# The intra-chunk score products of a hybrid token mixer: low levels by quarters into a compact tile, in five groups

## The reference, cut to what matters

```python
b = cumsum(gi, axis=2)                                   # log decay, one per channel
rel_decay = where(causal, exp(b[:, :, :, None] - b[:, :, None]), 0)
scores  = einsum('bhid,bhjd,bhijd->bhij', qi, ki, rel_decay)
o       = einsum('bhij,bhje->bhie', scores, vi) + einsum('bhcd,bhde->bhce', qi * exp(b), state)
state   = state * exp(b_last)[..., None] + einsum('bhcd,bhce->bhde', ki * exp(b_last - b), vi)
```

## Time and profile before

| | |
|---|---|
| median of 3 runs | 2037.15 us |
| profiled execution | span 2040.4 us from the first to the last instruction; no time of its own beside the span is given |
| TensorE busy | 1925.7 us (94%) |
| VectorE busy | 1472.5 us (72%) |
| chunk 0 of the mixers | 608.23 to 660.34 us of the span |
| chunks 1 to 6 | 660.34 to 1009.49 us |
| VectorE, all 56 copies of the levels' scores | 50.0 us |

### The profile page before, as it was taken

How to read it: one execution, slowest core, us unless ns; L and a number is a source line. 1 busy time by engine, 2 the same in 40 slices (tenths; PEclk the granted TensorE clock), 3 DMA queues, 4 the chain that set the end, 5 groups by cost and what they waited for, 6 DMA issues and landing times. The chain is left out here.

```text
span 2040.4 us, 26797 instructions
## 1 busy us (share of the span) xinstructions
PE 1925.7 (94%) x10602; PEld 1576.7 (77%) x10603; DVE 1472.5 (72%) x1687; ACT 1048.0 (51%) x1234; POOL 218.3 (11%) x173
## 2 busy tenths in 40 slices
PE   6999999999999999999998999995999999999993
PEld 5789888888977777777776888874788888888881
DVE  5876467667227888788775656556889988999875
ACT  5234344444224545444444334223777887888763
POOL 3310000000030000000001000012122222222210
PEclk9999999999999999999998999997999999999996
DMA  5242332432355557656537654543999999999986
GB/s 168 86 145 73 114 104 97 131 104 93 107 145 158 151 160 168 167 127 152 160 115 282 206 204 182 229 178 138 349 376 384 389 386 385 389 386 387 387 331 259
DMA packets 212415, 436.11 MB, mean 214 GB/s; under 512 B 28018, under 2 KB 151042, under 8 KB 184770
## 3 DMA queue, kind: packets, MB, share of 16 engines
q1 hardware_dynamic: 179394, 355.68, 50.3%
q10 hardware_dynamic: 20864, 53.49, 7.5%
q0 software_dynamic: 12032, 25.22, 3.2%
HBM read 369.67 MB, written 81.43 MB: 221 GB/s over the span
## 5 line engine op out<-in xcount | busy, mean ns | idle before, releaser
L1602 PE MATMUL psum<-h_hi,l_hi 128*128 128x512 f32 x384 | 158.5, 413 | 4.9 <-PEq L58 3.3
L1602 PE MATMUL psum<-h_lo,l_hi 128*128 128x512 f32 x384 | 159.8, 416 | 0.0
L1602 PE MATMUL psum<-h_hi,l_lo 128*128 128x512 f32 x384 | 157.9, 411 | 0.0
L2741 DVE TENSOR_TENSOR gu_lo<-up_raw,gu_hi 128x2048 fp32r<-128x2048 f32 x64 | 146.3, 2288 | 13.2 <-ACT gu_hi L2684 13.2
L2684 ACT CAST gu_hi<-up_raw 128x2048 fp32r<-128x2048 f32 x64 | 122.1, 1909 | 35.0 <-PE u_ps L2813 35.0
L1258 ACT COPY l_out<-psum 128x512 f32<-128x512 f32 x48 | 28.1, 585 | 170.3 <-PE psum L1602 162.3
L2457 PE MATMUL mpsum<-y_hi,wb_hi 128*128 128x512 f32 x256 | 103.3, 403 | 10.1 <-DVE y_lo L2217 9.1
L2813 PE MATMUL g_ps<-gu_hi,xeT_hi 128*128 128x512 f32 x256 | 105.0, 410 | 5.8 <-DVE xeT_lo L2750 5.8
L806 DVE TENSOR_TENSOR w_lo<-w_raw,w_hi 128x512 fp32r<-128x512 f32 x90 | 61.9, 689 | 65.5 <-ACT w_hi L662 65.5
L662 ACT CAST w_hi<-w_raw 128x512 fp32r<-128x512 f32 x90 | 55.7, 622 | 91.9 <-PE ps L931 91.4
L2457 PE MATMUL mpsum<-y_lo,wb_hi 128*128 128x512 f32 x256 | 101.7, 397 | 0.0
(11 more groups left out here) (465 smaller groups left out, 5419.0 us busy)
## 6 DMA issues: line engine op xcount, KB each, us to landing
up_raw<-moe SPq DMA_DIRECT2D x62, 1024.0 KB, 8.1
gate_raw_a<-moe SPq DMA_DIRECT2D x33, 1024.0 KB, 8.4
gate_raw<-moe SPq DMA_DIRECT2D x33, 1024.0 KB, 8.4
dn_raw_a<-moe SPq DMA_DIRECT2D x31, 1024.0 KB, 7.2
dn_raw<-moe SPq DMA_DIRECT2D x31, 1024.0 KB, 8.0
w_raw<-w_in SPq DMA_DIRECT2D x26, 1024.0 KB, 6.1
l_raw<-w_gates ACTq DMA_DIRECT2D x24, 512.0 KB, 5.4
s_gates<-l_out ACTq DMA_DIRECT2D x48, 256.0 KB, 4.0
```

Source lines behind the costliest of these rows:

```text
L1602: ins = nc.tensor.matmul(psum[:, bank, :], w[t % 2][:, k, :], x[:, k, half * 512:half * 512 + 512], start=i == 0, stop=i == LATE_MM - 1, s ...
L2741: nc.vector.tensor_tensor(gu_lo[p][:], gu_raw[p][:], gu_hi[p][:].bitcast(F32), ALU.subtract).then_inc(gu_ready, 1)
```

## The change: what it does

1. **Five groups instead of nine.** Levels 1 and 2, 3 and 4, and 5 and 6 are put next to each other on TensorE, with one semaphore step for both; the diagonal is one step. The late products that stood between them are in longer stretches: 8, 24, 16, 16, 8, 16 before the transposes of k, where it was 8 eight times and then 16. There are still 120 in a chunk.
2. **Quarters.** Levels 2 to 6 and the diagonal are computed for 4 quarters of 32 keys instead of 2 halves of 64: 24 matmuls with 32 weight columns, of 16 (or twice 16) moving columns. Level 1 has its two blocks of 32 keys. Level 0 stays.
3. **A compact tile.** Levels 2 to 6 and the diagonal are copied under a mask into `near` [128, 8, 32] instead of `score`: 128 columns a level and 256 for the diagonal. The blocks of levels 0 and 1 go into `score` by plain copies (1 of 64 partitions, 2 of 32).
4. **GpSimd** then moves the four diagonal blocks of `near` into `score`, four copies of 32 partitions x 8 x 32 a chunk, and the output product waits for them as well (`near_moved`).
5. **Order.** On VectorE the diagonal comes first and factors 1 after it; factors 3 and 4 come right ahead of `cbm`, `dec` 6 and 7 and `late(h0)` behind it. On TensorE `ssm_state` comes right after B.C, and `ssm_means` after the transposes of B, with levels 3 and 4 behind them. At the start of the stage five masks are built instead of seven, each reduced to one quarter.

```diff
+    SLOT_OF = (1, 2, 2, 3, 3, 4, 4)
+    COL_OF = (0, 0, 256, 0, 128, 0, 128)
+    NS = SLOT_OF[-1] + 1
...
+            for c in range(NCH):                     # GpSimd
+                pool.wait_ge(score_ready, NS * (c + 1))
+                for r in range(4):
+                    rs = slice(r * QUART, (r + 1) * QUART)
+                    nc.gpsimd.tensor_copy(score[rs, :, rs], near[rs, :, :]).then_inc(near_moved, 1)
...
+                def far_in(lv):                      # VectorE
+                    s, at, h = SLOT_OF[lv], COL_OF[lv], LEVELS[lv]
+                    dve.wait_ge(sc_ready, NS * c + s + 1)
+                    if c:
+                        dve.wait_ge(o_ready, c)
+                    for k in range(0, CH, 2 * h):
+                        ins = nc.vector.tensor_copy(score[k:k + h, :, k + h:k + 2 * h],
+                                                    sc_ps[s % 2][k:k + h, at:at + NH * h].rearrange("p (a h) -> p a h", h=h))
+                    if lv == 0:
+                        ins.then_inc(score_ready, 1)
+                def near_in(lv):
+                    s, at, h = SLOT_OF[lv], COL_OF[lv], LEVELS[lv]
+                    dve.wait_ge(sc_ready, NS * c + s + 1)
+                    v = lambda x: x.rearrange("p (n h) -> p n h", h=h)
+                    ins = nc.vector.copy_predicated(near[:].rearrange("p a (n w) -> p (a n) w", w=2 * h)[:, :, h:2 * h],
+                                                    v(mask[lv][:]), v(sc_ps[s % 2][:, at:at + NH * QUART // 2]))
+                    if lv % 2:
+                        own.link(ins)
+                    else:
+                        ins.then_inc(score_ready, 1)
+                        dve.wait_ge(score_ready, NS * c + s + 1)
...
                 factors(0)
+                diagonal_in()
+                dec(i0 + 3)
                 factors(1)
...
-                scores_in(2)
-                dec(i0 + 6)
+                far_in(1)
+                near_in(2)
+                factors(3)
                 factors(4)
-                late(h0)
                 dve.wait_ge(cb_ready, c + 1)
                 tt(cbm[:], ...)
+                dec(i0 + 6)
+                dec(i0 + 7)
+                late(h0)
                 if c:
                     ssm_state(c - 1)
-                scores_in(3)
-                dec(i0 + 7)
+                near_in(3)
+                near_in(4)
                 factors(5)
                 late(h0 + 1)
-                scores_in(4)
                 factors(6)
                 ... # xdt, dec 8, k and q of the state as before
-                scores_in(6)
+                near_in(5)
+                near_in(6)
...
             def level(c, lv):                        # TensorE
+                s, at, h = SLOT_OF[lv], COL_OF[lv], LEVELS[lv]
+                n = NS * c + s
                 pe.wait_ge(qk_ready, NE * c + lv + 1)
-                pe.wait_ge(score_ready, NS * c + lv + 1)
+                if n > 1:
+                    pe.wait_ge(score_ready, n - 1)
+                rows, cols, each = (h, h, 2 * h) if lv < FIRST_MASK else (QUART, QUART // 2, QUART)
+                out = sc_ps[s % 2][:, at:at + NH * cols].rearrange("p (a n) -> p a n", n=cols)
                 for a in range(CT):
+                    head, q2 = pairs_of_heads(ql, a)
+                    for i, k in enumerate(range(0, CH, each)):
+                        ins = nc.tensor.matmul(out[k:k + rows, head:head + q2.shape[1], :],
+                                               k_lv[lv % 2][:, a * CH + k:a * CH + k + rows],
+                                               q2[:, :, i * cols:(i + 1) * cols], start=True, stop=True, skip_group_check=True)
+                if lv % 2 == 0:
+                    ins.then_inc(sc_ready, 1)
...
                 level(c, 0)
-                fill(SLOT)
+                fill(3 * SLOT)
                 level(c, 1)
-                fill(SLOT)
                 level(c, 2)
                 ... # B.C of the SSM
-                fill(SLOT)
-                level(c, 3)
                 if c:
                     ssm_state(c - 1)
-                fill(SLOT)
-                if c:
-                    ssm_means(c - 1)
+                fill(2 * SLOT)
                 pe.wait_ge(cbm_ready, c + 1)
                 ... # transposes of B
-                fill(SLOT)
+                if c:
+                    ssm_means(c - 1)
+                level(c, 3)
                 level(c, 4)
-                fill(SLOT)
+                fill(2 * SLOT)
                 ... # transposes of x
                 fill(SLOT)
                 level(c, 5)
-                fill(SLOT)
                 level(c, 6)
                 fill(2 * SLOT)
...
                 pe.wait_ge(score_ready, NS * c + NS)
+                pe.wait_ge(near_moved, 4 * c + 4)
```

More of the change, by code:

```diff
@@ L1003, in mixers @@
         mask_f = sb("mask_f", [P, HALF])
-        mask = many(NL, "mask", [P, NH * HALF], U8)
-        mask_d = sb("mask_d", [P, 4 * CH], U8)
+        mask_q = sb("mask_q", [P, QUART])
+        mask = {lv: sb(f"mask{lv}", [P, NH * QUART // 2], U8) for lv in range(FIRST_MASK, NL)}
+        mask_d = sb("mask_d", [P, NH * QUART], U8)
         tri = sb("tri", [P, CH])
@@ L1050, in mixers @@
         score_ready = sem("score_ready")
+        near_moved = sem("near_moved")
         eb6_ready = sem("eb6_ready")
@@ L1215, in _ @@
             n = 0
[L1216 removed]
+            for lv in range(FIRST_MASK, NL):
+                h = LEVELS[lv]
                 nb = CH // (2 * h)
[L1218 to L1219 removed]
+                if lv > FIRST_MASK:
+                    pool.wait_ge(mask_ready, lv - FIRST_MASK)
                 nc.gpsimd.memset(mask_f[:], 1.0).then_inc(mask_sem, 1)
@@ L1502, in body @@
                     late(3)
-                scores_in(0)
+                far_in(0)
                 factors(2)
+                dec(i0 + 5)
                 if c:
                     intra_in(c - 1, 1)
[L1507 to L1510, removed]
                     x_weighted(c - 1)
@@ L1613, in heads, with pairs_of_heads @@
                     yield GLA_HEADS + h, 4 + h, 2 + h, slice(0, P)
+            def pairs_of_heads(q, a):
+                return (2 * a, q[:, a:4:2, :]) if a < 2 else (a + 2, q[:, a + 2:a + 3, :])
             def level(c, lv):
+                s, at, h = SLOT_OF[lv], COL_OF[lv], LEVELS[lv]
+                n = NS * c + s
                 pe.wait_ge(qk_ready, NE * c + lv + 1)
-                pe.wait_ge(score_ready, NS * c + lv + 1)
+                if n > 1:
+                    pe.wait_ge(score_ready, n - 1)
                 ql = q_lv[lv % 2][:].rearrange("p (a n) -> p a n", n=HALF)
-                out = sc_ps[lv % 2].rearrange("p (a n) -> p a n", n=HALF)
+                rows, cols, each = (h, h, 2 * h) if lv < FIRST_MASK else (QUART, QUART // 2, QUART)
+                out = sc_ps[s % 2][:, at:at + NH * cols].rearrange("p (a n) -> p a n", n=cols)
                 for a in range(CT):
[L1623 to L1629, removed]
+                    head, q2 = pairs_of_heads(ql, a)
[5 more added lines that the diff above has]
+                    ins.then_inc(sc_ready, 1)
             def diagonal(c):
@@ L1636, in diagonal @@
                     pe.wait_ge(inter_used, c)
[L1637 to L1642, removed]
-                    ins.then_inc(sc_ready, 1)
+                out = sc_ps[0][:, 0:NH * QUART].rearrange("p (a n) -> p a n", n=QUART)
+                for a in range(CT):
+                    head, q2 = pairs_of_heads(q_in[b], a)
+                    for r in range(4):
+                        rs = slice(r * QUART, (r + 1) * QUART)
+                        ins = nc.tensor.matmul(out[rs, head:head + q2.shape[1], :], k_in[b][:, a, rs], q2[:, :, rs],
+                                               start=True, stop=True, skip_group_check=True)
+                ins.then_inc(sc_ready, 1)
             def ssm_state(c):
@@ L1729, in body @@
                 for h, qa, a, r in heads():
-                    nc.tensor.matmul(o_ps[:, h * CH:(h + 1) * CH], v_in[:, h, :], score[:, h * CH:(h + 1) * CH], start=True, stop=False)
+                    nc.tensor.matmul(o_ps[:, h * CH:(h + 1) * CH], v_in[:, h, :], score[:, h, :], start=True, stop=False)
                     ins = nc.tensor.matmul(o_ps[:, h * CH:(h + 1) * CH], state[:, a, :], q_in[b][:, qa, :], start=False, stop=True)
```

48 lines of the change are left out of this document (21 added, 27 removed).

## The result

| | before | after |
|---|---|---|
| median of 20 runs, us | 2037.64 | 2046.16 |
| lowest to highest | 2034.06 to 2045.44 | 2039.36 to 2052.72 |
| ratio, 95% interval | | 1.0029 (1.0019 to 1.0039) |
| profiled execution: span, granted clock | 2040.4, 0.975 | 2045.0, 0.969 |
| mixers, first diagonal to last (chunks 0 to 6), us | 401.3 | 400.8 |

A forecast was written before the change was run, and what follows sets the result against it. TensorE's own list, plus waits at the transposes of B, was taken as the bound. Seven chunks at 2.4 us less (16.8) plus chunk 0's 3.1 made 20 us: 2037 to 2017, range 2003 to 2033, the forecast's own 2008 to 2026.

The forecast's parts named there:

- B at T+22.0: TensorE reaches the transposes of B 22.0 us after the chunk's start, when the chain load, `wd`, `cbm` ends.
- a second part of 32.1 before the clock: From the transposes of B to the next chunk, TensorE's list takes 32.1 us, from 33.7 without the clock's 1.7.
- chunk 0's 3.1 of gain: Chunk 0, without earlier SSM work or a wait for `cbm`, gains 3.1 us through levels, alternations and a shorter stop.
- A level's cost: Levels 2 to 6 on TensorE: 12 sets of four matmuls take 0.50 us a level instead of 0.82.
- records, not columns: Rival: a matmul record costs 34 ns in any width, a level 1.64 us; 2055, mild form 2041; chance 0.13.
- four no faster than two: Rival: four narrow matmuls side by side gain nothing, a level stays at 0.82 us; 2028; chance 0.13.
- TensorE idles 2.8 there, as today: Ahead of the transposes of B, TensorE is ready at 19.2 us but waits 2.8 us for `cbm`.
- the clock's 1.7: Half-clock TensorE behind the wait at the transposes of B: 1.7 us lost, charged to every chunk.
- The two alternations: Behind the transposes of B, two switches between late products and small groups go, saving 0.6 us at 0.3 each.
- the stop in the late products stands in place of its second wait, 0.3 less: Chunk 0: a 0.8 us stop among 24 late products replaces a 1.1 us wait for `l_out`, 0.3 less.
- cost 0: GpSimd's four copies, some 1.7 us a chunk, end before TensorE's output products ask, so they cost nothing.
- GpSimd late: Rival: GpSimd copies excluded by VectorE's multiplication end 0.8 us after TensorE asks; 6 us in seven chunks, 2023; chance 0.10.

The follow-up runs named there:

- e15: e13 with VectorE's copies of levels 5 and 6 ahead of the multiplications of k and q: 2012.2 us, ratio 0.9877.
- e1: The changed kernel with `wd` and its wait for `load_bb` behind `cbm` on VectorE: 2027.4 us, ratio 0.9933.
- e10: The changed kernel with the late products dealt 8, 16, 24 instead of 8, 24, 16 in chunk 0 alone: 2035.9 us, ratio 0.9979.
- e13: e8 with ScalarE's copy of the second half also sooner, ahead of the two wide exponentials: 2045.9 us, ratio 1.003.
- e9: The kernel before the change, unedited, profiled once more: one execution, 2033.6 us, its mixers 395.4 us.
- e3: The changed kernel without the four GpSimd copies and the waits for them, those score blocks missing from its result: 2040.3 us, ratio 1.0006.
- both edits: The changed kernel with `wd` and its load wait behind `cbm`, and late products dealt 8, 16, 24 in all chunks: 2023.4 us, ratio 0.992.
- e8: The kernel with both edits, ScalarE's copy of the half ending ahead of the transposes of B moved before W's first eight differences: 2022.6 us, ratio 0.9914.
- e11: The kernel with both edits, on VectorE `cbm` ahead of level 4's factors and the intra products' sum ahead of `dec` 5: 2022.5 us, ratio 0.992.
- e12: The kernel with both edits, without the four GpSimd copies and their waits, those score blocks missing from its result: 2021.2 us, ratio 0.9911.

## Why the prediction was wrong

Forecast: eight chunks 20 us shorter in all, 17.5 of them in the 401.3 us of chunks 0 to 6. Measured there: 401.2 on average of two profiles. The waits and the cost of the packed matmuls were foreseen; what failed are three terms of the sum, B at T+22.0, a second part of 32.1 before the clock, and chunk 0's 3.1 of gain, and the single profile that it started from.

- **A level's cost: right.** 0.50 a level was forecast. Levels 3 and 4 together take 1.01 (the 96 records from 684.36 to 685.37 in e15's chunk 1), levels 5 and 6 1.02; the diagonal takes 0.66 against 0.53. A level's records are 11 ns apart. The Trainium skill, "TensorE: Matmul & The Clock Gate", section "Wait — 56ns, not 53.3ns?", has a floor near 25 ns, by which the change would have been lost at once; for these records, four tiles side by side, the measurement decides against it. The rivals "records, not columns" and "four no faster than two" are out.
- **The first part, T to B: the step "TensorE idles 2.8 there, as today".** B was put at T+22.0, and came at T+21.0 to 23.8, 22.6 on average of seven, with 3.3 us of waiting each. Three of the seven lie beyond the T+23 that the forecast had named as a sign of being wrong. The transfer was issued 0.2 later than forecast (T+1.8), took 14.9 to 17.7 us, 16.5 on average, instead of 16.3, and the chain behind `wd` 4.3 instead of 4.1. Each is a small miss, and together they are 0.6 a chunk, 4 us: the mechanism was foreseen and its size nearly. What was missed is a question that was not put: what it would be worth to take `wd` out of the chain. e1: 17 to 19 us.
- **The second part: the step "That makes 32.1".** With the clock's 1.7, 33.8 was forecast; 34.6 was measured (six chunks), 5 us in all. The two chunks of the changed kernel in which the clock stayed at 1.00 behind B have 33.2, so the list was 1.1 too short. Today's list was put at 33.7, and chunk 5 before the change, at a clock of 1.00, has 34.0. The means cost 1.8 instead of 1.3. The two alternations gave 0.4 instead of 0.6. The clock cost less than forecast, 1.4 on average instead of 1.7: nothing in two chunks, about 1.6 in two, and over 2 in chunks 5 and 6, where it stayed low for twice as long.
- **Chunk 0: the step "the stop in the late products stands in place of its second wait, 0.3 less".** The stop was priced at 0.8 by a copy that waits for nothing. In chunk 4 it costs 0.93 (`l_out` waited for 0.77), so that was right; in chunk 0 ScalarE stood before the copy for its earlier store (1.43 us of idling) and TensorE waited 2.67. With the 3.58 us stop in level 5, which nothing had announced, chunk 0 is 4.1 us longer instead of 3.1 shorter. e10 shows that dealing chunk 0's late products otherwise takes both away: 9 to 10 us by the medians, 7 in chunk 0 of its profile.
- **GpSimd: "cost 0", right for the wrong reason.** TensorE did not wait for the copies. 1.7 us in all was forecast for them, done 2.5 us ahead of need. The copies take 3.8 and end at B+18.65 in chunk 4 (879.95), 0.4 us ahead of the output products. e13 took that reserve away and lost 23 us. The rival "GpSimd late" had the mechanism, and its chance of 0.10 was too small for whoever edits next.
- **The base.** The sum was taken off one profile whose mixers were 6 us longer than in the second profile of the same kernel (e9), 3 longer than the average of the two. A sum of 20 us should have carried such differences in its range.

By sizes: 4 (first part), 5 (second part), 7 (chunk 0) and 3 (the base) are 19 of the 28 to 29 us between 2017 and the medians of 2044.7 and 2046.2. 1 to 3 more are the starting point, 2037 from three runs where later series had 2037.6 to 2040.2. The last 6 to 9 are not placed; the stage begins up to 6 us earlier or later from one profile to the next (607.6 to 613.9), in both kernels alike.

What makes the stop of 3.58 us in level 5 is open as well. It stood in two profiles of the changed kernel and in e3, and in none that deals chunk 0's late products 8, 16, 24, though the levels are as dense there; so density alone is not it. e1 keeps the old dealing and has no such stop, but there TensorE waited 2.40 us for ScalarE's copy behind levels 3 and 4, and its chunk 0 is as long. No experiment isolates the cause.

## What to carry to other kernels

When a stage is a chain through a transfer, shorten nothing on it before looking which instruction waits for the transfer, and who is only queued behind that one: moving a `wd` of 0.17 us gave 17 us or more, and without that move some 2 us a chunk less of TensorE's work gave nothing. Keep two profiles of the kernel before when the effect is a few us a stage: here they differed by 6. Edits that each give nothing may be three queues that hold one point in turn; take them together (beside both edits, e8, e11, e12 and e13 gave 1, 1, 2 and -23 us, of which only the last is clear of none, and e15, one move more than e13, 11). Whatever is put on GpSimd beside a busy VectorE wants a reserve for each VectorE instruction that it can meet: the four copies took 6.0 us in chunk 0 of the changed kernel and 5.2 in two chunks of e15, where several of them met one.

## What the runs showed of the hardware that was not expected

A GpSimd copy of 32x256 takes 0.39 us alone and 2.44 us when VectorE's 2.29 us multiplication of two SBUF operands stands beside it. The changed kernel, chunk 4, the first, third and fourth copy, and that multiplication:
```profile
876.15 0.39 POOL L1249 COPY score<-near 32x256 f32<-32x256 f32 x1 [54.41 <-DVE near L1515]
...
877.05 2.44 POOL L1249 COPY score<-near 32x256 f32<-32x256 f32 x1
...
879.55 0.40 POOL L1249 COPY score<-near 32x256 f32<-32x256 f32 x1
...
876.94 2.29 DVE L1578 TENSOR_TENSOR dn_raw_a<-dn_raw_a,cbm 128x2048 f32<-128x2048 f32 x1 [0.85 <-ACT dn_raw_a L1338]
```
The third copy ends 0.26 us after the multiplication does (879.49 and 879.23). By the rule of the Trainium skill, "SBUF — State Buffer", section "SBUF: two separate sides", that the two exclude each other for a whole instruction, the trace agrees. In e15 both engines pay, in turn: VectorE's multiplication of k begins at 694.66, beside a copy that ends at 695.05, and takes 1.20 us instead of 0.95; the next copy begins at 695.10 and ends at 696.11, 0.25 us after the multiplication.
